# Trunk of a hybrid decoder step in two parts of tokens, with the expert rows of two blocks fetched beside the second

## The reference

```python
A = window_attention(q, k, v, ...)      # window 128, 16 heads, 4 kv heads, T5 bias, sinks
# RWKV-7, 16 heads of 64, one step for each token, in order:
sa = einsum("bhvk,bhk->bhv", S, kk_t)
S  = S * w_t - sa * kka_t + v_t * k_t ;  y_t = S @ r_t
mix = (sigmoid(gate_attn)*(A @ w_branch_attn) + sigmoid(gate_rwkv)*(B @ w_branch_rwkv)) @ w_out
h = LayerNorm(alpha * x + mix)
# PEER, for each token and each of 8 heads: top 16 of 128 scores on two sides, top 16 of the sums
act = gelu(einsum("bhkd,bd->bhk", peer_u[eidx], xb))     # 128 experts for each token
y = LayerNorm(alpha * h + einsum("bhk,bhkd->bd", gate * act, peer_v[eidx]))
```

## Time and profile before

| stage | from, us | length, us |
|---|---|---|
| project_plain | 0 | 451 |
| project_pairs | 451 | 483 |
| scan_pairs | 934 | 712 |
| attend | 1646 | 319 |
| decode | 1965 | 81 |
| merge | 2046 | 235 |
| fronts | 2281 | 775 |
| experts | 3056 | 1974 |

### The profile page before, as it was taken

One profiled execution on the slowest core, in us unless ns is written; L12 is line 12 of the kernel. 1 busy time (PEld: TensorE's weight loads), 2 busy tenths in 40 slices (PEclk: granted clock), 3 DMA queues, 4 the chain that ended last, 5 costly groups with the idle time before them and its releaser, 6 DMA issues. The chain is left out here.

```text
span 5030.4 us, 74255 instructions
## 1 busy us (share of the span) xinstructions
PE 4244.3 (84%) x28493; PEld 2644.9 (53%) x28493; DVE 3199.9 (64%) x6337; ACT 767.7 (15%) x1239; POOL 1314.1 (26%) x1213
## 2 busy tenths in 40 slices
PE   8998999698987375897577764999999999999995
PEld 5665666587876264665365641444444444444441
DVE  0001676344444245112988895999899989999996
ACT  0111222121211143100222330000000000010000
POOL 0000010000000000000000002666666766676663
PEclk9999999899988687898788987999999999999996
DMA  2212333312110510323212225999999999999995
GB/s 102 76 68 74 107 127 121 129 46 75 58 50 28 147 20 24 104 79 126 88 69 95 93 96 225 384 396 364 386 392 395 378 389 396 376 394 388 390 329 194
DMA packets 315419, 977.97 MB, mean 194 GB/s; under 512 B 37067, under 2 KB 93989, under 8 KB 312016
## 3 DMA queue, kind: packets, MB, share of 16 engines
q0 software_dynamic: 176432, 649.40, 33.7%
q1 hardware_dynamic: 129268, 307.58, 17.2%
q10 hardware_dynamic: 9420, 16.87, 0.9%
HBM read 854.99 MB, written 120.95 MB: 194 GB/s over the span
## 5 line engine op out<-in xcount | busy, mean ns | idle before, releaser
L1898 PE MATMUL x_vps<-x_v,x_w 128*128 128x512 f32 x2048 | 905.2, 603 | 54.0 <-DVE x_w L2052 54.0
L1888 PE MATMUL x_sps<-k_hT,x_u 128*128 128x512 f32 x2048 | 887.4, 595 | 74.9 <-DMA x_u<-u_cols 74.8
L1853 POOL DMA_INDIRECT x_ring<-u_rows,k_eidx x512 | 655.9, 1281 | 561.3 <-DVE x_dots L2017 349.3
L2035 DVE SCALAR_TENSOR_TENSOR x_yacc<-x_ring,x_wts,x_yacc 128x1024 f32<-128x1024 f32 x512 | 657.9, 1285 | 73.2 <-DMA x_ring<-v_rows,k_eidx 56.7
L1898 PEld LDWEIGHTS x_vps<-x_v,x_w 128*128 128x128 f32 x2048 | 395.5, 194 | 561.0 <-issue 494.5
L1888 PEld LDWEIGHTS x_sps<-k_hT,x_u 128*128 128x128 f32 x2048 | 389.8, 191 | 569.5 <-issue 487.4
L2017 DVE CUSTOM_DVE_ANT_0 x_ring<-x_ring,x_h 128x1024 f32<-128x1024 f32 x512 | 600.0, 1224 | 33.7 <-DMA x_ring<-u_rows,k_eidx 31.3
L1853 POOL DMA_INDIRECT x_ring<-v_rows,k_eidx x512 | 541.4, 1057 | 191.2 <-issue 148.3
L137 PE MATMUL pzp<-c_xT,pw 128*128 128x344 f32 x1440 | 422.0, 454 | 18.1 <-DMA pw<-w_tiles 16.8
L257 PE MATMUL qzp<-c_xT,qw 128*128 128x344 f32 x1152 | 345.1, 460 | 18.7 <-DVE q_hc L382 18.7
L137 PEld LDWEIGHTS pzp<-c_xT,pw 128*128 128x128 f32 x1440 | 272.8, 191 | 161.5 <-DMA pw<-w_tiles 16.8
(11 more groups left out here) (394 smaller groups left out, 5717.2 us busy)
## 6 DMA issues: line engine op xcount, KB each, us to landing
x_u<-u_cols SPq DMA_DIRECT2D x128, 512.0 KB, 7.5
x_v<-v_rows SPq DMA_DIRECT2D x128, 512.0 KB, 13.2
s_G<-f_stage POOLq DMA_DIRECT2D x16, 2048.0 KB, 8.3
x_G<-s_G SPq DMA_DIRECT2D x16, 2048.0 KB, 27.8
r_in<-s_rw SPq DMA_DIRECT2D x56, 512.0 KB, 7.4
s_rw<-q_out POOLq DMA_DIRECT2D x48, 512.0 KB, 4.1
s_zT<-pz ACTq DMA_DIRECT2D x30, 516.0 KB, 3.7
pw<-w_tiles SPq DMA_DIRECT2D x30, 512.0 KB, 3.9
```

Source lines behind the costliest of these rows:

```text
L1853: pool.indirect_dma_start(out=ring[:, r, :], out_offset=None, in_=A[table], in_offset=bass.IndirectOffsetOnAxis(ap=eidx[n // SLOTS][:, n % ...
L1888: mm = pe.matmul(sps[n % 2][:, :], u[n % 4][:, k, :], hT[:, k, :], start=(k == 0), stop=(k == KT - 1))
L1898: mm = pe.matmul(vps[m % 2][:, x * 512:(x + 1) * 512], w[:, e, k * P:(k + 1) * P], v[:, e, x * 512:(x + 1) * 512], start=(e == 0), stop=(e ...
L2035: mark(V.scalar_tensor_tensor(ya[:, :], ring[:, q % RING, :], wts[:, s:s + 1], ya[:, :], ALU.mult, ALU.add), S["used"], q + 1)
```

## The change

The trunk (the six stages ahead of `fronts`) runs twice, for a `Part` of the tokens each: first 384 tokens (blocks 0, 1, 2) without `decode`, then 640 tokens with the 8 decoded ones. Groups of columns become one of 384, and two of 324 (325 where the token ahead is needed). All of the weights of the trunk are loaded once for each part; the scan's state stays in SBUF (`c_STc`); hardware loops are written out as straight code. `attend` makes its table in the first part alone.

Between the parts, `fronts` runs for blocks 0, 1, 2 and chooses experts for block 0. During the second trunk, the class `Rows` fetches and sums blocks 0 and 1: 64 groups in the queues of SP, Pool, ACT and DVE, dealt by the plan `beside` (19 in `project_plain`, 8 in the pairs, 16 in the scan, 5 in `attend`, 12 in `merge`, 10 turns behind it, of which 4 are whole groups and the rest sums alone). A `dve` slot is one dot, or one sum from 4 groups earlier, in the engine's order.

Then `fronts` runs for blocks 3 to 8. Its choice for the next block now stands between the 32 turns of `scatter`; each turn makes its one-hots in two instructions of 128x512, and ACT multiplies one of them by the gates (4 instructions a turn). In `experts`, blocks 2, 3, 4 are dense (384 tokens) and blocks 5, 6, 7 are fetched: 6 groups a chunk, 4 in the S phase, one behind each of the first two dense blocks of the V phase. 

```diff
+EARLY = [0, 1, 2]
+FETCHED_1 = [0, 1]
+DENSE = [2, 3, 4]
+FETCHED_2 = [5, 6, 7]
+ND = len(DENSE)
...
+PARTS = [Part("e_", 0, WIN * len(EARLY), False), Part("l_", WIN * len(EARLY), NP - WIN * len(EARLY), True)]
...
+    def fetch(self, pool, table, n, q):
+        r, s = q % self.RING, n % SLOTS
+        idx = self.A["sb_eidx"][self.blocks[n // SLOTS]]
+        if q >= self.RING:
+            pool.wait_ge(self.S["used"], q - self.RING + 1)
+        stand_alone(pool, self.A)
+        pool.indirect_dma_start(out=self.ring[:, r, :], out_offset=None, in_=self.A[table],
+                                in_offset=bass.IndirectOffsetOnAxis(ap=idx[:, s:s + 1], axis=0)).then_inc(self.got[r], 16)
...
+    def dve(self, dve, n):
+
+        self.ch.dve = dve
+        for s in range(self.dve_at, min(self.dve_at + n, 8 * self.TOTAL)):
+            g, x = s // 8, s % 8
+            if x < 4 and g < self.NGT:
+                self.dot(dve, 4 * g + x)
+            if x == 3 and 0 <= g - self.LAG_W < self.NGT:
+                self.weights(dve, g - self.LAG_W)
+            if x >= 4 and 0 <= g - self.LAG_V < self.NGT:
+                self.add(dve, 4 * (g - self.LAG_V) + x - 4)
+            if x == 7:
+                self.rest(dve, g // self.NG, g % self.NG)
+        self.dve_at += n
...
+            bg.dve(dve, 8 * sum(plan["groups"](u) for u in range(N_PLAIN)))
...
+                bg.dve(dve, 4 * plan["pair"])
...
+                    bg.dve(dve, plan["dve0"](c))
...
+                    bg.dve(dve, plan["dve1"](c))
...
+                    bg.dve(dve, plan["unit"])
...
+                    bg.dve(dve, 4 * plan["group"](i))
...
+            bg.dve(dve, 8 * plan["rest"])
...
+            def weigh(n, q):
+                act.wait_ge(S["one_done"], n + 1)
+                for t in range(PER):
+                    c = PER * q + t
+                    mm = act.activation(two[q % 2][:, t, :], two[q % 2][:, t, :], ACT.Copy, scale=byslot[:, 2, c:c + 1])
+                mm.then_inc(S["two_done"], 1)
...
-                        V.tensor_scalar(one[q % 2][:, t, :], T["iota"][:, :], byslot[:, 0, c], None, ALU.is_equal)
-                        ins = V.tensor_scalar(two[q % 2][:, t, :], T["iota"][:, :], byslot[:, 1, c], byslot[:, 2, c], ALU.is_equal, ALU.mult)
...
+                wide = T["iota"][:, :].unsqueeze(1).broadcast_to([P, PER, NKEY])
+                V.tensor_tensor(one[q % 2][:, :, :], wide, byslot[:, 0, c].unsqueeze(2).broadcast_to([P, PER, NKEY]), ALU.is_equal)
+                V.tensor_tensor(two[q % 2][:, :, :], wide, byslot[:, 1, c].unsqueeze(2).broadcast_to([P, PER, NKEY]), ALU.is_equal).then_inc(S["one_done"], 1)
...
+                for q in range(TURNS):
+                    scatter(k, q)
+                    if k + 1 < NPK:
+                        choose(k + 1, q)
...
+        before = lambda e: 1 if e % 2 and e // 2 < PERC else 0
+        behind = lambda k: len(range(CH // 2 + k, PERC, ND))
...
+    beside = {"groups": lambda u: 1 if u >= 4 and u % 4 else 0, "pair": 1, "turn": 2, "act": lambda c: 1 if c in (4, 9) else 0,
+              "dve0": lambda c: 1 if c not in (3, 8) else 0, "dve1": lambda c: 1 if c not in (3, 8) else 0,
+              "block": 1, "unit": 2, "group": lambda i: 1 + i % 2, "rest": 20}
...
+        trunk(PARTS[0], none, nothing)
...
+        fronts(nc, A, "e_", EARLY, FETCHED_1[:1], [])
...
+            bg = Rows(nc, A, sb, c3.enter_context(signals(nc, "l_")), FETCHED_1, FETCHED_1[1:] + [None], [], 10, 3, 4)
+            trunk(PARTS[1], bg, beside)
...
+        fronts(nc, A, "l_", [b for b in range(NB + 1) if b not in EARLY], DENSE + FETCHED_2[:1], DENSE)
```

More of the change, by code:

```diff
@@ L50 @@
 N_RW = 7
+PH, NKEY, TOPK = 8, 128, 16
+SLOTS = PH * TOPK
+CAND = [(i, TOPK // (i + 1)) for i in range(TOPK)]
+NCAND = sum(n for _, n in CAND)
+LOW = -3.0e38
+EARLY = [0, 1, 2]
[3 more added lines that the diff above has]
+ND = len(DENSE)
+CH = 8
+NCH = NKEY // CH
+TGW = 32
 class Steps:
@@ L120, in _, with natural @@
+            if pt.first:
+                sp.wait_ge(const_in, 48)
         @block.tensor
         def _(pe):
[L122 to L142, removed]
+            def natural(u):
+                j = u % 2
+                pe.wait_ge(z_sbuf, u + 1)
+                if u >= 2:
+                    pe.wait_ge(t_sbuf, u - 1)
+                pe.transpose(tp[j][0:NS + 1, 0:P], z[j][:, pt.n - 1:N], ident[:, :]).then_inc(t_psum, 1)
@@ new lines, in _, with project_pairs @@
+        @block.gpsimd
+        def _(pool):
+            bg.pool(pool, sum(plan["groups"](u) for u in range(N_PLAIN)))
+        @block.vector
+        def _(dve):
+            bg.dve(dve, 8 * sum(plan["groups"](u) for u in range(N_PLAIN)))
+def project_pairs(nc, A, pt, bg, plan):
+    dec = pt.dec
+    only = lambda *names: names if dec else ()
+    PE = Steps("w", "a", "g", "r", "ss", "v", "bonus", *only("raw_t", "dec_t"))
+    AC = Steps("w", "a", "g", "r", "Dinv", "D", "Dprev", *only("wdec"), "norm", "v", *only("raw_t", "dec_t0", "dec_t1"))
+    DV = Steps("k_d", *only("k_ds"), "k_f", "kkr", "sq", "lw", "scan", "lprev", "a", "ka1", "kp",
+               "r_d", *only("r_ds"), "r_f", "rkr", "rk", "ssm", "rinv", "kk", "kka", "v_d", *only("v_ds"), "v_f",
@@ new lines, in scan_pairs @@
+    on_act = dict((x, e == "A") for x, e in prep)
+    slot_of = {x: i % 2 for i, x in enumerate(order)}
+    PER = -(-len(order) // NC)
+    FIRST = -(-PER // 2)
+    early = lambda c: [g for g in range(PER * c, PER * c + FIRST) if g < len(order)]
+    late = lambda c: [g for g in range(PER * c + FIRST, PER * c + PER) if g < len(order)]
+    assert len(order) % 2 == 0 and MID * NY == NC
+    last = f"Y{NY - 1}"
+    chain = [x for c in range(NC) for x in ((f"u{c}", "Y0", f"s{c}") if NY == 2 and c == MID else (f"u{c}", f"s{c}"))] + [last]
@@ L531, in scan_pairs, with state @@
         tok = lambda g: slice(g * HT, (g + 1) * HT)
-        EARLY = [n for n in range(N_RW) if n != R_RHO]
-        def turns(engine, turn):
-            turn(0, 0, False, True)
-            with engine.Fori(0, NPAIR // 2 - 1) as i:
-                turn(2 * i + 1, 1, True, True)
-                turn(2 * i + 2, 0, True, True)
-            turn(NPAIR - 1, (NPAIR - 1) % 2, True, False)
+        tokens = slice(pt.t0, pt.t0 + n)
+        EARLY_IN = [i for i in range(N_RW) if i != R_RHO]
+        def state(c, p, o):
+            if c == 0 or (c == NC and not dec):
+                return STc[o, p, :]
+            return ST[o, col(c)]
@@ L568, in _ @@
+            store(NPAIR - 1)
+            for j in range(2):
+                sp.wait_ge(y_out[j], 16 * (NPAIR // 2))
         @block.tensor
@@ L792, in store, with attend @@
[L792 to L805 removed]
+            bg.pool(pool, plan["turn"] * NPAIR)
+def attend(nc, A, pt, bg, plan):
```

2087 lines of the change are left out of this document (1116 added, 971 removed).

## The result

The changed kernel has a median of 5065.99 us (5064.35 to 5069.7, 4 runs); its ratio to the kernel before, which has a median of 5037.38 us over the four runs beside it, is 1.0059 (interval 1.0041 to 1.0076): slower by 0.6%. The forecast was 5008 us, faster by 0.6%. The time lies within the stated range, but the kernel became slower where it was to become faster.

The account below looks back on a forecast made before the run. PE was taken to bound the stages up to 3056 us and transfers the experts. Experts -366, trunk +281 and fronts +56 sum to -29: span 5001, execution 5003, timed 5008 us; range 4880 to 5110.

Parts of the forecast that it names:

- What bounds the kernel: PE sets the pace up to 3056 us, DVE about half busy; experts bound by transfers, falling 366 us to 1608.
- Part one: First trunk run, 384 tokens without rows: stages scaled with their columns plus fixed ends, together 919 us.
- Early fronts: Fronts for blocks 0 to 2: second norm and scores, three asks, a choice and ends, 179 us.
- Part two, pairs and plain: Second trunk with rows beside: pairs 362 us, their end set by DVE, 295 without it; plain 287, rows hidden.
- The scan: Second scan: 443 us plus a sixth of the slots' 162 us of DVE, 27, makes 470; bounds 443 and 605.
- the rival of slots ahead of the chain: Slots delay the scan's and pairs' links: scan 550 us, total 5098, deciding from 36 us beyond the 27; chance 0.2.
- The merge: Second merge: 69 MB of transfers take 182 us, over PE's 141; with the last groups 260, bounds 225 and 275.
- A merge bound by the Pool's waits: Listed among the profile signs that would show the forecast wrong; no size given.
- Late fronts: Fronts for blocks 3 to 8: 3.7 us a scatter turn, 119.5 a block, DVE idle during mixes and asks; 652 us.
- The tables of ACT: Some 25 more table switches in pairs, scan and attention, 32 us of ACT; only the links' 6 us summed.
- a chunk near 100: Experts' chunks stay near 100 us because S and V don't fill each other; total 5104, deciding from 96; chance 0.12.
- rows at next to no cost: Slots fall into DVE's idle trunk time and experts reach the bytes' limit, 92 us a chunk; near 4870, chance 0.2.

Follow-up runs that it names:

- the early square root: Changed kernel with ACT taking the square root of block 2's norm before block 1's scores; 5049.2 us in one run, early fronts 177.1.
- without rows: Changed kernel with nothing beside the second trunk, blocks 0 and 1 of the retrieval left out; 4746.4 us.
- the early fetches: Changed kernel with Pool issuing group i+1's fetches in merge before tile i's sum and store; median 5018.7 us, ratio to the kernel before 0.9965.
- the old scatter: Changed kernel with the previous scatter (eight 128x128 one-hots a turn, no ACT weighing), next block's choice behind it; 5001.1 us, ratio to before 0.9933.

## Why the prediction was wrong

- **What bounds the kernel**: right for the experts, as far as the runs show. Fewer bytes, columns and groups took 387 us out (366 predicted), at 93.5 us a chunk against 94, with the DMA busy 0.97; that the order within a chunk sets part of it isn't excluded. The reading that DVE is busy about half up to 3056 us was too coarse: it is busy 0.02 of 451 us in plain and 29.6 of 235 in the merge.
- **Part one**: 864 for 919. Each stage was scaled too high, attend most (142.6 for 164): its first product began 51.4 us after the barrier (677.7 - 626.3), where the 65 us of the earlier trace rows were kept as fixed, and its 12 units took 91 us where 99 were allowed. The 13.9 us for a tile of plain should have been 14.2 ((451 - 25)/30), which would have made the stage 176, not 172; it measured 169.6.
- **Early fronts**: 197 for 179. The order on ACT was not read against the third norm; the run with the early square root gives the 179 back.
- **Part two, pairs and plain**: 366.4 for 362 and 291.7 for 287. DVE sets the pairs' end as said (322.7 of 366.4 busy), and without rows they take 321.0, not 295: the rows' cost was 45 us and not 67, and the trunk itself dearer.
- **The scan**: 512.2 for 470. This step failed as well. The mechanism was named, its size taken at a sixth of the slots' 162 us, 27; the rows cost 76 there. Without rows the scan took 436.4, where 443 was predicted. This is the rival of slots ahead of the chain, at 49 us over the forecast's share, beyond its point of decision at 36. Its own 550 us counted the forecast's 27 twice: half of 1.3 us for each of 128 slots is some 80 on 443, which is 523, near the measured 512.
- **The merge**: the step that failed by itself and turned the sign. "12 groups are 50 MB, with 19 of its own 69 MB, 182 us, over PE's 141": the stage was costed by its resources, and its queue was not walked. The fetches stand behind a store that waits for the engine that the fetches feed, and the stage took 318.7 us. The prediction's bounds, 225 and 275, left it out; the early fetches bring it to 268, within them. "A merge bound by the Pool's waits" did stand among the signs of being wrong, but no rival gave it a price.
- **Late fronts**: 661.3 for 652, the arithmetic right for what was built (119 us for a block's turns, 119.5 predicted), and the moved choice named as the cause of DVE's idle gaps. What was not worked out is that the old scatter and order would take 75 us less. That "338 us of one-hots become 133" sets four blocks against three; for three they were 253.
- **The sign**: the forecast gain of 29 us was smaller than the merge's miss of 59 and the scan's of 42. The merge's 51 us alone turn it: with the early fetches the kernel is 0.35% faster than before.
- **The tables of ACT**: the prediction put them at some 25 more loads and left them out of the sum. Part two has 86 with the rows and 18 without, 68 more, 87 us of ACT at 1.28 each (below); 50 of them are in the pairs, the scan and attend, for which the 25 were meant. What they cost the stages by themselves was not tried: it lies within the 313 us.
- **Rivals**: a chunk near 100 and rows at next to no cost are refuted by the experts at 93.5 us and by the run without rows, by which the rows cost 313.

## What to carry to other kernels

When work is woven into queues that wait for each other, follow one turn round: what each engine issues, what stands ahead of it, and whether a prefetch stands behind a store that waits for the consumer of that very prefetch. Cost a background slot by the queue and the place in it; here the same group cost 0.5 us in a stage bound by PE and 12.5 with nothing beside it. A piece of work that fills an engine while the bound engine waits is worth more than one that fills it while it is busy anyway: the choice was moved out of the only gap that it had filled.

## What the hardware showed

ACT's loads of a table were many more than expected. The group of the rows' Gelu, in part two of the changed kernel:

```profile
L339 ACT ACT_TABLE_LOAD x37 | 47.5, 1283 | 6.5 <-ACT l_q_decn L735 5.7 <-ACT l_pzn L512 0.4
```

Behind most of these ACT loads the stage's own table again: in the scan 15 loads for the Gelu stand beside 15 for the stage's square root, and in the run without rows the scan has no load. Between two instructions of ACT in part two a load looks like this:

```profile
1423.88 0.71 ACT L708 ACTIVATE l_qz<-l_qzp 128x650 f32<-128x650 f32 x1 [9.58 <-PE l_qzp L637]
1424.61 1.28 ACT L710 ACT_TABLE_LOAD   x1
1425.91 0.74 ACT L710 ACTIVATE l_q_Di<-l_q_lcum 128x640 f32<-128x640 f32 x1
```

The load begins 0.02 us behind the one and ends 0.02 us ahead of the other, so the switch takes 1.3 us here. The Trainium skill (ScalarE: Activation LUTs, What ACT_TABLE_LOAD costs) puts a switch at 2.66 us with its drain; this trace doesn't agree, and the measurement decides.

The granted clock fell in a stage where PE is not idle but works in short bursts: the late fronts of the changed kernel were granted 0.66, with turns of 3.05 us and more, and 0.79 with the old scatter:

```profile
2822.80:3409.60 586.80, 360.36 (x1977) 284.13 (x1977) 485.78 (x1799) 135.96 (x138) 17.46 (x18) 0.79 0.25 96
```

In the scan the same 10336 matmuls were busy for 399.2 us at a granted clock of 0.86 with the rows beside, and for 376.7 at 0.90 without:

```profile
1661.70:2098.10 436.40, 376.74 (x10336) 349.83 (x10336) 196.49 (x360) 105.54 (x168) 0.00 (x0) 0.90 0.20 64
```

So the lower clock shows as 22 us more of busy PE in a scan that is 76 longer. Whether these lie on the chain was not tried.

The Trainium skill (DMA: Bandwidth & Descriptors, Specifications) gives about 358 GB/s of HBM for a core; the core moved 384 GB/s over 1400 us of the experts and 412 over 90 us of the merge with the early fetches, so here the measurement decides, as it did before the change.
